# Half-row blocks of 512 columns, a new order of fills, and a fold by transposes in a four-layer transformer kernel

## The chip, the cores and the metric

One NeuronCore of one Trainium2 chip runs the whole program. The metric is the device time of one execution in microseconds; the time of a kernel is the median of its runs. Everything is float32. "TensorE", "VectorE", "ScalarE" and "GpSimd" are the PE, DVE, ACT and POOL of the profile; SP issues the weight transfers.

## The reference

Two blocks of two layers each work on x of 256 tokens by 1024. A layer of the first kind (layers 0 and 1):

```
h = x @ w_in                                  # dq dk dv sq sk sv iq ik iw ga gb
ya = rms_norm(diff_attention(dq, dk, dv, lam))         # 4 heads, two softmaxes each
score = sum_h relu(iq_h . ik) * iw_h                   # index search: 64 keys per query
yb = attention(sq, sk, sv) over the chosen keys        # "dsa", 8 heads
mix = (sigmoid(ga) * (ya @ w_bd) + sigmoid(gb) * (yb @ w_bs)) @ w_o
x = layer_norm(ALPHA * x + mix)
ffn = 2 of 32 experts per token: (silu(x @ w_g) * (x @ w_u)) @ w_d
x = layer_norm(ALPHA * x + ffn + sigmoid(x @ w_ple_gate) * (p @ w_ple))
```

A layer of the second kind (two more):

```
p = rms_norm(x) @ w_in_2                      # cq ckv kr mq mk mv rq rk rv rg g0 g1 g2
o_mla, o_moba = two causal attentions, 8 heads;  o_ret = retention, 4 heads
x = x + (sum of sigmoid(g) * (o @ w_branch)) @ w_out_2
x = x + relu(rms_norm(x) @ w_up)**2 @ w_down
```

The weights are some 420 MB and are read once.

## The kernel before, in words

**One plan, five programs.** `Plan` (L98) writes out the order of all steps; each engine then walks the same list (`for s in plan.steps`) and emits its share of each step, so the order of the plan is the order on every engine and on SP's queue. Within an engine everything is in order; between engines there are semaphores with counted names.

**The weight stream.** The weights are laid out in the order of use, in blocks of up to 128 x 2048 (1 MB). `take` (L163) appends a block: it emits `fetch` (SP's DMA into the next free tile of `self.buffers`) and, for blocks that aren't raw, `split`: ScalarE casts to a high half (L1778), VectorE subtracts it (L1264) to get the low half, each in two pieces of 1024 columns, into one of three pairs WS (`PAIRS`). Splits are emitted up to two blocks ahead. Three ring tiles carry the stream; `lend` (L150) adds a dead tile at the head of the list, with the work that must be over before the first transfer into it, and `recall` takes it back. Before, PT and H are lent when the experts start, GT and V0 from expert 8 on. The experts' down weights are raw: TensorE reads them as float32 from the tile.

**Matmuls.** `mm3` forms each product as three fp32r matmuls (high x high, high x low, low x high). A `tok` step (L945, helper line L916) keeps 128 tokens as the stationary operand and streams 256 columns of w: one block is all eight 128-row slices of 256 columns, one PSUM bank holds both token halves. `gate`, `ret_gate` and `mlp_up` keep the weights stationary and stream 256 tokens. Four banks (`bank_free`: a step waits until the bank used four banks ago is emptied) and scp hold the outputs; `owner` says whether ScalarE or VectorE empties a bank, and `turn` (transposes in groups of four, L993) alternates between them (`either`).

**Fills.** `self.todo` is a list of blocks of TensorE work that wait for nothing (gates, branches); `fill(n)` runs n of them, and `attend` (L231) takes three counts: how many behind the first half's softmax, behind the second's, and before the last product. `self.spare` holds small VectorE steps (index search: 54 per layer; routing; slot weights), of which `pace` are emitted after every `take`.

**A first-kind layer** (L261): iq, ik, sq, sk, then index scores; dq, dk, dv, sv with 9 index steps behind each block; `turn` ST and DT (the transposed q and k); attention "diff"; its output is turned and split (`turn_split` oa, into FA), attention "dsa" follows with the branches and the gates gb as fills; `turn_split` ob, the last branch, `merged` (the sum is split into FA in four pieces, L1526), w_out, `load_p` (the split of p into FA, L1531), norm ln1, ple, `turn_split` ln1, router, ple_gate with the routing behind it, gather, 32 experts. An expert e: two blocks of gate and up weights for 64 tokens, high halves in rows 0 to 63 and low halves in rows 64 to 127 of the stationary operand, so the bank holds 64 high and 64 low rows of 512 outputs; ScalarE copies it (SE, L1920); `turn_h` (L1136) multiplies the copy by the constant "fold" (ones at r and r + 64), which transposes it and adds the two halves in one float32 matmul; ScalarE takes the tanh (L1916), VectorE forms the product (L1686, L1688), and `down` follows under the next expert. `tokens_of` prepares the next expert's tokens (L1913, L1681).

**A second-kind layer** (L392): norm, cq (256 + 160 columns), mq, mk, q_up, kv_up, mv, rv, rq; attentions "mla" and "moba", retention "ret", with gates, ret_gate and branches as fills; `turn_split` o0, o1, o2; the last branch, `merged`, w_out_2, norm, and the MLP in four quarters.

## Time and profile before

| | before |
|---|---|
| median of 3 runs | 2198.76 us (2197.55 to 2204.66) |
| the profiled execution | 2194.55 us, span 2192.7 us |
| mean granted clock of TensorE | 0.954 |
| busy: PE, DVE, ACT, POOL | 93%, 62%, 49%, 5% of the span |
| stream | 421.65 MB in the SP queue, mean 195 GB/s with all else |

The profile gives busy times per engine, what each idle time waited for, and the chain of work that ended last. A wait is put down to the last releaser. Matmul starts are exact; their ends are modelled, so spacings are read from start to start. Most matmuls have the one helper line L916 and are told apart by their tiles: WSh and WSl are the halves of a weight block, XTh and XTl those of the tokens, FA holds split operands, SC the experts' copy and the attention's probabilities. Layers begin near 0, 617, 1227 and 1706 us; experts run from 318 to 588 and from 922 to 1191 us.

### The profile page before, as it was taken

What the parts mean: (1) busy time and instruction counts of PE and PEld (TensorE: products, weight loads), DVE (VectorE), ACT (ScalarE), POOL (GpSimd) and SP (SyncE); (2) the same over time, 40 slices, a digit from 0 to 9 for tenths busy, and PEclk for the clock granted to TensorE, in tenths of its full rate; (3) what the DMA queues carried; (4) which work ended last, traced back from release to release, by engine and by line L of the source; (5) the groups of instructions that cost most, each with busy time, mean ns of one, the idle gap of its engine ahead of it and who ended that gap; (6) DMA issues with size and microseconds to landing.
All of it is one profiled execution on the core that took longest, in us unless ns stands there. A gap on an engine that the chain in (4) does not pass through costs nothing.

```text
span 2192.7 us, 35340 instructions
## 1 busy us (share of the span) xinstructions
PE 2032.7 (93%) x14696; PEld 1920.4 (88%) x14696; DVE 1366.4 (62%) x2230; ACT 1069.1 (49%) x1662; POOL 102.1 (5%) x88
## 2 busy tenths in 40 slices
PE   7979899999989798999999799888999898989998
PEld 7979889999889798899998798888989898988897
DVE  4775668677647756686776555566444655665444
ACT  4443456667534434566675344434444544434443
POOL 1000020000010000200000000000000000000000
PEclk9989889999989998999999799999999999989999
DMA  6423339999624233399996153333555343334552
GB/s 247 155 96 132 111 155 381 392 391 388 233 92 160 96 128 113 150 383 391 389 391 244 58 184 116 105 141 134 181 192 186 136 154 116 127 125 152 192 185 84
DMA packets 60184, 426.95 MB, mean 195 GB/s; under 512 B 6849, under 2 KB 7249, under 8 KB 9200
## 3 DMA queue, kind: packets, MB, share of 16 engines
q1 hardware_dynamic: 59040, 421.65, 52.2%
q8 instruction: 119, 1.95, 0.4%
q0 software_dynamic: 400, 1.75, 0.3%
q10 hardware_dynamic: 576, 1.19, 0.1%
q14 instruction: 49, 0.40, 0.0%
HBM read 423.52 MB, written 1.05 MB: 194 GB/s over the span
## 4 chain that ended last, share of the span: by engine, by line
PE 86%; DVE 8%; ACT 4%; issue 1%; DMA 1%; POOL 0%; DVEq 0%; ACTq 0%; POOLq 0%; SPq 0%
PE bank L916 72%; PE scp L916 10%; DVE WSl L1264 1%; ACT SC L1812 1%; PE bank L1008 1%; PE bank L1035 1%; PE bank L993 1%; ACT WSh L1778 1%; DVE sm L1401 0%; POOL sm L1979 0%; PE bank L1160 0%; DVE scp L1399 0%; DMA ring<-wts 0%; DVE sm L1247 0%; DMA H<-wts 0%
## 5 line engine op out<-in xcount | busy, mean ns | idle before, releaser
L1264 DVE TENSOR_TENSOR WSl<-ring,WSh 128x1024 fp32r<-128x1024 f32 (+3 forms) x560 | 650.5, 1203 | 236.0 <-ACT WSh L1778 234.6
L1778 ACT CAST WSh<-ring 128x1024 fp32r<-128x1024 f32 (+3 forms) x560 | 549.4, 1033 | 178.4 <-PE scp L916 87.7
L916 PE MATMUL bank<-WSh,FA 128*128 128x256 f32 (+1 forms) x1168 | 332.8, 342 | 21.0 <-DVE FA L1526 8.8
L916 PE MATMUL bank<-XTh,WSh 128*128 128x256 f32 x1216 | 348.5, 287 | 0.1
L916 PE MATMUL bank<-XTl,WSh 128*128 128x256 f32 x1216 | 345.4, 284 | 0.0
L916 PE MATMUL bank<-XTh,WSl 128*128 128x256 f32 x1216 | 345.2, 284 | 0.0
L916 PE MATMUL bank<-WSh,XTh 128*128 128x256 f32 (+3 forms) x1024 | 300.9, 294 | 13.8 <-DVE WSl L1264 12.2
L916 PE MATMUL bank<-WSl,XTh 128*128 128x256 f32 (+3 forms) x1024 | 298.3, 291 | 0.0
L916 PE MATMUL bank<-WSh,XTl 128*128 128x256 f32 (+3 forms) x1024 | 297.8, 291 | 0.0
L916 PE MATMUL bank<-WSl,FA 128*128 128x512 f32 (+1 forms) x840 | 297.4, 354 | 0.0
L916 PEld LDWEIGHTS bank<-WSh,FA 128*128 128x128 f32 x1168 | 204.4, 195 | 43.1 <-issue 9.5
L916 PEld LDWEIGHTS bank<-XTh,WSh 128*128 128x128 f32 x1216 | 235.0, 193 | 1.6 <-issue 1.2
L916 PEld LDWEIGHTS bank<-XTl,WSh 128*128 128x128 f32 x1216 | 234.9, 193 | 0.2
L916 PEld LDWEIGHTS bank<-XTh,WSl 128*128 128x128 f32 x1216 | 234.6, 193 | 0.0
L916 PEld LDWEIGHTS bank<-WSh,XTh 128*128 128x128 f32 x1024 | 207.4, 202 | 16.0 <-DVE WSl L1264 12.2
L916 PEld LDWEIGHTS bank<-WSl,XTh 128*128 128x128 f32 x1024 | 207.6, 203 | 0.0
L916 PEld LDWEIGHTS bank<-WSh,XTl 128*128 128x128 f32 x1024 | 207.1, 202 | 0.0
L916 PEld LDWEIGHTS bank<-WSl,FA 128*128 128x128 f32 x840 | 162.9, 194 | 19.2
L916 PE MATMUL bank<-FA,WSh 128*128 128x256 f32 x640 | 129.8, 305 | 32.0 <-DVE FA L1507 14.2
L916 PE MATMUL scp<-WSh,FA 128*128 128x512 f32 x512 | 159.0, 389 | 0.0
L916 PEld LDWEIGHTS bank<-FA,WSh 128*128 128x128 f32 x640 | 110.3, 212 | 35.0 <-issue 31.3
L916 PEld LDWEIGHTS scp<-WSh,FA 128*128 128x128 f32 x512 | 96.1, 188 | 19.7
(263 smaller groups left out, 2853.6 us busy)
## 6 DMA issues: line engine op xcount, KB each, us to landing
ring<-wts SPq DMA_DIRECT2D x296, 1024.0 KB, 4.9
PT<-wts SPq DMA_DIRECT2D x34, 1024.0 KB, 7.3
GT<-wts SPq DMA_DIRECT2D x26, 1024.0 KB, 7.3
H<-wts SPq DMA_DIRECT2D x24, 1024.0 KB, 8.4
V<-wts SPq DMA_DIRECT2D x16, 1024.0 KB, 8.9
ring<-wts SPq DMA_DIRECT2D x2, 768.0 KB, 4.3
ring<-wts SPq DMA_DIRECT2D x2, 640.0 KB, 4.3
X<-x POOLq DMA_DIRECT2D x1, 1024.0 KB, 5.8
```

The costliest lines, as they stand in the source:

```text
L916: return nc.tensor.matmul(dst, lhsT, rhs, start=start, stop=stop)
L993: last = nc.tensor.transpose(bank[u % 4][0:s.w, j * P:(j + 1) * P], src, ident)
L1008: last = nc.tensor.transpose(bank[u % 4][:, j * P:(j + 1) * P], src(t, c), ident)
L1035: last = nc.tensor.transpose(bank[u % 4][:, (j - s.first) * P:(j - s.first + 1) * P], p_at(j // nk)[:, j % nk * P:(j % nk + 1) * P], ident)
L1264: nc.vector.tensor_tensor(lo[:, c], buf[:, c], hi[:, c].bitcast(F32), ALU.subtract).then_inc(*lo_done.inc(("block", i)))
L1778: nc.scalar.copy(hi[:, c], buffers[s.buffer][:, c]).then_inc(*hi_done.inc(("half", i, k)))
L1812: ins = nc.scalar.activation(SC[:, h, 0:kl], scp[:, h, 0:kl], ACT.Exp, bias=nb[t][:, h:h + 1], scale=SCALE[s.name], accum_out=zs[t][:, h:h ...
```

## The change

- `wide`: a group of 512 output columns in two blocks, each four of the eight 128-row slices ("half-row blocks"), into two banks, one per 128 tokens. All `columns`, ple_gate, w_out and cq (416 columns) use it; copies and tanh, and the update of X with its statistics (chunks of 512), follow.
- sv leaves the stretch of the index search and becomes two items of `todo`; `pace` there is 13.
- New counts: dsa (2, 2, 1), mla (2, 1, 1), moba (2, 2, 1); some blocks are kept behind the transposes of ob, o0, o1 and o2.
- `merged` in two halves of its own tiles of FA, w_out starting with the first; `load_p` between the two column groups of w_out, into XT.
- `turn_split` of ln1, ln2 and o2 in groups of two pairs: first both affine steps, then both splits.
- `turn_h` by four transposes; VectorE adds the halves (a reduction out of PSUM into GU) before the tanh.
- YA, YB (QKT), V1 and PT are lent from the second attention of a first-kind layer on; YA and YB come back at expert 1, V1 at expert 27, with waits (`held`) for the last block in them. GpSimd's memset shrinks and its sum into V1 moves to a step `keep`.

```diff
-    def lend(self, name, lender):
+    def lend(self, name, lender, at=0):
         self.lent.add(name)
-        self.buffers.insert(0, (name, lender))
+        self.buffers.insert(at, (name, lender))
+    def wide(self, w, name, l, c, c0, n, src, owner="act", row=None, **fields):
+        u = []
+        def block(h):
+            i = self.take((w, (l if row is None else row,), 4 * h, 4, c0, c0 + n))
+            if h == 0:
+                u.extend(self.bank(owner) for _ in range(T))
+            self.add("wide", name=name, l=l, c=c, h=h, n=n, i=i, u=u, src=src, **fields)
+            self.release(i)
+        return [lambda: block(0), lambda: block(1)]
...
-        self.pace = 9
+        self.pace = 13
         self.columns("w_in", "dk", l, W1["dk"], 512, src)
         self.add("rope", name="dq", l=l)
         self.columns("w_in", "dv", l, W1["dv"], 512, src)
-        self.columns("w_in", "sv", l, W1["sv"], 512, src)
         self.no_more_than(0)
         self.pace = 1
         self.todo.extend(self.gates("w_in", l, "ga", W1["ga"], src))
+        self.todo.extend(self.wide("w_in", "sv", l, 0, W1["sv"], 512, src))
...
-        self.attend("dsa", l, 8, (1, 2, 1), diff_out)
-        self.fill(9)
+        self.attend("dsa", l, 8, (2, 2, 1), diff_out)
+        for name in ("YA", "YB"):
+            self.lend(name, ("pe", "scores", "dsa", l, 1, 1), at=RING)
+        self.lend("V1", ("pe", "attended", "dsa", l, 1), at=RING)
+        self.lend("PT", ("pe", "PT", self.use("PT", "pe") - 1), at=RING)
+        self.fill(len(self.todo) - 1)
         fa = self.use("FA", "pe")
         self.turn_split("ob", l, 4, o=self.now("O"), fa=fa)
-        for f in self.branch("w_branch_dsa", l, "ob", "gb", fa):
-            f()
+        self.fill(9)
+        blocks = self.branch("w_branch_dsa", l, "ob", "gb", fa)
+        blocks[0]()
+        self.add("merged", l=l, stage=1, last="ob", h=0, fa=None)
+        blocks[1]()
         fa = self.use("FA", "pe")
-        self.add("merged", l=l, stage=1, last="ob", fa=fa)
+        self.add("merged", l=l, stage=1, last="ob", h=1, fa=fa)
...
-        self.attend("mla", l, 8, (1, 2, 1))
+        self.attend("mla", l, 8, (2, 1, 1))
         self.turn("MT", l, 16, P)
-        self.fill(9)
+        self.fill(1)
...
-        self.attend("moba", l, 8, (1, 2, 1), mla_out)
-        self.fill(9)
+        self.attend("moba", l, 8, (2, 2, 1), mla_out)
...
-        self.fill(9)
+        self.fill(len(self.todo) - 2)
         fa = self.use("FA", "pe")
         self.turn_split("o2", l, 4, o=o, fa=fa)
+        self.fill(9)
...
-                        last = mm(bank[u % 4][:, f * CAP:(f + 1) * CAP], SE[s.e % 2][:, f * P:(f + 1) * P], const("fold"), True, True)
+                        last = nc.tensor.transpose(bank[u % 4][:, f * P:(f + 1) * P], SE[s.e % 2][:, f * P:(f + 1) * P], ident)
...
+                    both = bank[u % 4][:, :].rearrange("p (f h s) -> p f s h", f=4, h=2)
+                    dve.wait_ge(pe_done, "bank", u)
+                    nc.vector.tensor_reduce(v.rearrange("p g f s -> p (g f) s"), both, AX.X, ALU.add).then_inc(*dve_done.inc(("bank", u), ("folded", l, s.e)))
                     dve.wait_ge(act_done, "silu", l, s.e)
...
-                    act.wait_ge(pe_done, "bank", u)
+                    act.wait_ge(dve_done, "folded", l, s.e)
```

## Rows read from the trace of the kernel before

**Rows 1.** Page, part 1: engine, busy us (share of the span) xinstructions.
```profile
PE 2032.7 (93%) x14696; PEld 1920.4 (88%) x14696; DVE 1366.4 (62%) x2230; ACT 1069.1 (49%) x1662; POOL 102.1 (5%) x88
```

**Rows 2.** Page, part 4: shares of the chain that ended last, by engine.
```profile
PE 86%; DVE 8%; ACT 4%; issue 1%; DMA 1%; POOL 0%; DVEq 0%; ACTq 0%; POOLq 0%; SPq 0%
```

**Rows 3.** Waits of PE: for what; us in total, times, longest us.
```profile
PE bank L916 <- DVE FA L1507: 14.2, 6, 4.9
...
PE bank L916 <- DVE FA L1495: 9.1, 4, 3.0
PE bank L916 <- DVE FA L1526: 8.8, 4, 2.2
PE bank L916 <- DVE FA L1502: 8.8, 2, 4.4
...
PE bank L1008 <- ACT GT L1891: 7.0, 4, 1.9
...
PE scp L916 <- ACT SC L1812: 5.8, 2, 2.9
PE bank L916 <- DVE FA L1531: 4.4, 2, 2.2
```

**Rows 4.** Chain in order of time: start us, us, what, matmuls.
```profile
111.53 1.75 PE bank L993 x16
...
1565.86 23.03 PE bank L916 x192
1588.89 21.79 PE scp L916 x96
```

**Rows 5.** Timeline of PE, cq's 160 columns, first and last of 48.
```profile
1236.57 0.24 PE L916 MATMUL bank<-WSh,XTh 128*128 128x160 f32 x1
...
1241.79 0.28 PE L916 MATMUL bank<-WSh,XTl 128*128 128x160 f32 x1
```

**Rows 6.** Timeline of PE, one expert: start us, us, operation.
```profile
439.50 3.68 PE L916 MATMUL bank<-TMP,V 128*128 128x64 f32 x32
443.01 1.06 PE L916 MATMUL bank<-CST,SC 128*128 128x64 f32 x8
443.88 0.48 PE L916 MATMUL bank<-WSh,FA 128*128 128x512 f32 x1
```

**Rows 7.** Timeline of DVE, a reduction from PSUM.
```profile
123.02 0.69 DVE L1401 TENSOR_REDUCE sm<-scp 128x4 f32<-128x512 f32 x1
```

**Rows 8.** Timeline of DVE in the experts.
```profile
366.14 1.22 DVE L1711 SCALAR_TENSOR_TENSOR X<-GT,X 128x1024 f32<-128x1024 f32 x1
...
441.76 0.68 DVE L1681 TENSOR_TENSOR FA<-A,FA 128x512 fp32r<-128x512 f32 x1
...
444.74 0.29 DVE L1688 SCALAR_TENSOR_TENSOR TMP<-TMP,bank 128x128 f32<-128x128 f32 x1
```

**Rows 9.** Timeline of PE, the expert after those pieces.
```profile
368.02 0.50 PE L916 MATMUL bank<-WSh,FA 128*128 128x512 f32 x1 [0.70 <-DVE FA L1681]
```

**Rows 10.** Stretches of the experts: busy PE, PEld, DVE, ACT, POOL, PEclk, DMA share, GB/s.
```profile
440.00:548.00 108.00, 108.00 (x750) 99.28 (x750) 77.69 (x94) 74.54 (x107) 0.00 (x0) 1.00 0.99 389
380.00:404.00 24.00, 24.00 (x181) 22.54 (x180) 15.62 (x20) 14.51 (x23) 0.00 (x0) 1.00 1.01 418
```

**Rows 11.** Timeline of DVE around the index search of layer 0.
```profile
79.68 2.36 DVE L1264 TENSOR_TENSOR WSl<-ring,WSh 128x1024 fp32r<-128x1024 f32 x2 [6.61 <-ACT WSh L1778]
...
107.37 2.36 DVE L1264 TENSOR_TENSOR WSl<-ring,WSh 128x1024 fp32r<-128x1024 f32 x2 [0.79 <-ACT WSh L1778]
...
112.00 0.69 DVE L1436 COPY A<-bank 128x512 f32<-128x512 f32 x1
```

**Rows 12.** Stretches, columns as in Rows 10.
```profile
318.10:323.10 5.00, 5.00 (x13) 3.84 (x13) 3.48 (x3) 2.28 (x3) 3.60 (x2) 0.50 1.01 426
1310.00:1500.00 190.00, 172.00 (x1377) 167.41 (x1376) 117.30 (x195) 77.05 (x146) 2.03 (x2) 0.96 0.35 123
1790.00:1985.00 195.00, 177.19 (x1397) 172.42 (x1396) 121.26 (x201) 78.81 (x147) 2.04 (x2) 0.94 0.35 124
```

More of the change, by code:

```diff
@@ L67 @@
 C_TABLE = [("ident", 128), ("caus", 128), ("invf", 8), ("iota8", 8), ("nhalf", 8)]
-C1_TABLE = [("before", 128), ("one", 1), ("fold", CAP)]
+C1_TABLE = [("before", 128), ("one", 1)]
 C3_TABLE = [("iota", SLOTS)]
@@ L207, in turn_split @@
     def turn_split(self, name, l, n, at=0, **fields):
-        for j in range(2 * at, 2 * at + n, 2):
-            owner = "act" if name in ("ln1", "ln2", "o2") and j // 2 % 2 == 0 else "dve"
-            self.add("turn_split", name=name, l=l, j=j // 2, n=min(2, 2 * at + n - j), u=self.bank(owner), **fields)
+        pairs = range(2 * at, 2 * at + n, 2)
+        if name not in ("ln1", "ln2", "o2"):
+            for j in pairs:
+                self.add("turn_split", name=name, l=l, j=j // 2, n=min(2, 2 * at + n - j), u=self.bank("dve"), **fields)
+            return
+        for a in range(0, len(pairs), 2):
+            for j in pairs[a:a + 2]:
+                self.add("turn_split", name=name, l=l, j=j // 2, n=2, u=self.bank("dve" if j // 2 % 2 else "act"), **fields)
+            for j in pairs[a:a + 2]:
+                self.add("shifted_split", name=name, l=l, j=j // 2, n=2, **fields)
     def gates(self, w, l, g, c0, src):
@@ L317, in first_layer @@
         for c in range(4):
-            self.add("ple", l=l, c=c, i=i, u=self.bank("act"), gt=gt, fa=fa)
+            self.add("ple", l=l, c=c, i=i, u=self.bank("act"), gt=gt)
         self.release(i)
@@ L332, in first_layer @@
         self.pace = 0
+        blocks = [f for c in range(2) for f in self.wide("w_ple_gate", "ple_gate", l, c, 512 * c, 512, ("ln1", l))]
         for c, self.lead in enumerate((14, 20, 28, 0)):
+            if c == 2:
+                self.first("YA", "YB")
             if c == 3:
@@ L336, in first_layer @@
                 self.add("x_lo", l=l)
-            self.tok("ple_gate", l, c, ("w_ple_gate", (l,), 0, KD, c * 256, (c + 1) * 256), 256, src=("ln1", l))
+            blocks[c]()
             if c == 1:
@@ L1068, in tensor_program @@
                     if s.c == ends:
-                        names += [("read", i)] + ([("FA", s.fa)] if s.kind == "ple" else [])
+                        names.append(("read", i))
                     last.then_inc(*pe_done.inc(*names))
@@ L1265, in vector_program @@
                             *lo_done.inc(("block", i)))
-                elif s.kind == "tok" and s.name == "w_out":
-                    xs = X[:, :, s.c * 256:(s.c + 1) * 256]
-                    dve.wait_ge(pe_done, "bank", u)
+                elif s.kind == "wide" and s.name == "w_out" and s.h:
                     if l < DEPTH:
@@ L1934, in scalar_program @@
                     act.wait_ge(pool_done, "YC0", l)
+                    for block_, raw in plan.held["Y", l]:
+                        if raw:
+                            act.wait_ge(pe_done, "read", block_)
+                        else:
+                            act.wait_ge(lo_done, "block", block_)
                     if s.e:
```

178 lines of the change are left out of this document (112 added, 66 removed).

## Prediction

> **What bounds the kernel now.** I read the page's busy times first, then its chain by engine, the waits of TensorE, and last the timelines where the change cuts. TensorE is busy for 2032.7 of 2192.7 us [rows 1] and holds 86% of the chain that ended last [rows 2]. So a change gains in three ways: fewer microseconds of TensorE work, less idle time before it, and fewer stretches at half clock (the granted clock has two levels here, 1.0 and 0.5 [rows 12]). The idle time is 160 us; its largest removable parts stand in the waits: for the operand splits FA (L1507, L1495, L1526, L1502, L1531), for exp (L1812) and for freed banks (L1891) [rows 3]. Nothing smaller than 0.3% of the time (6.6 us) can be told from no change. The profiled execution took 2194.55 us (span 2192.7), 4.2 us under the median of 2198.76; I sum against it and add 4.2 at the end.
>
> **1. Blocks of 512 columns.** 192 matmuls of 256 columns take 23.03 us, 119.9 ns each; 96 of 512 take 21.79 us, 227.0 ns each [rows 4]. One of 512 replaces two of 256: 12.9 ns saved. A group of 512 output columns has 2 x 8 x 3 = 48 such pairs, 0.62 us. There are 11 groups in a first-kind layer (iq, sq, sk, dq, dk, dv, sv, w_out 2, ple_gate 2) and 7 in a second-kind one (mq, mk, mv, rv, rq, w_out 2): 36 in all, **-22.2 us**. The Trainium skill (TensorE: Matmul & The Clock Gate, Back-to-back issue gap) gives a back-to-back spacing of N/2.4 + 2.5 ns, so a fixed part of 2.5 ns; by it this term would be only 48 x 36 x 2.5 ns = 4.3 us. The rows show 13 ns over the columns' time, so the measurement decides. The copies by ScalarE keep their count of elements; cost nil, under 10.9 us of matmuls.
>
> cq was 256 + 160 columns and becomes 416. The 160-column matmuls start within 5.22 us, 47 intervals of 111.1 ns [rows 5], hardly faster than 256. Before: 48 x (119.9 + 111.1) = 11.1 us. After, between the rows for 256 and 512: 48 x 186.8 = 9.0 us. Two layers: **-4.2 us**.
>
> **2. Fold by transposes.** An expert takes 8.14 us on TensorE: 3.76 us of 512-column matmuls, 3.51 us down, and the fold, 8 records from 443.01 to the next expert at 443.88: 0.87 us [rows 6]. Four transposes replace it; 16 transposes take 1.75 us [rows 4], so 0.44 us. The period becomes 7.71 us if nobody else sets it; 64 x 0.43 = -27.5 us. What it costs VectorE: a reduction of 128x512 from PSUM, nearest row 0.69 us [rows 7]. The chain fold, reduce, tanh, two products grows from about 1.1 to 2.0 us and is hidden under the next expert's 3.76 us. But VectorE is in order: the four split halves and the next tokens are behind it. Now the tokens end at 442.44, 1.44 us before TensorE wants them [rows 8]. Later by 0.95 us and wanted 0.43 us earlier, they have 0.1 us left: TensorE just stays the bound. In experts 3 to 6 VectorE also forms slot weights and adds the ple part (pieces of up to 1.22 us [rows 8]; 1.6, 1.6, 2.4, 2.3 us per expert by the timeline). Today that costs one wait of 0.70 us [rows 9]. Then VectorE needs 4 x 7.0 + 7.7 = 35.7 us for what TensorE does in 30.8: 4.9 us less the slack, 4.5, in place of 0.9 lost now. That is 3.6 us per layer. Bounds of the period: 7.71 (TensorE) and 8.14 (no gain), or above where the reduction is slower than its row. Term: -27.5 + 7.2 = **-20.3 us**.
>
> **3. The stream.** At 7.71 us per expert the 3.15 MB need 408 GB/s. The DMA engines are busy for 0.99 of 440 to 548 us at 389 GB/s, but gave 418 GB/s where more transfers were queued [rows 10]. With eight tiles filled before the experts (three ring tiles, PT, V1, YA, YB, H), 88 of 96 blocks are left: at 389 GB/s 237 us, less than 32 x 7.71 = 247. So the lent tiles hide the roof and give nothing more by themselves: cost nil, bound +20.3 us if they don't. The Trainium skill (DMA: Bandwidth & Descriptors, the table of limits at its head) puts HBM at about 358 GB/s per core; the rows already go beyond that. SP's queue issues the same 402 blocks, and the waits for lenders come behind ring blocks already due. POOL's shorter memset and the later add (V) hide behind experts.
>
> **4. Fills in a first-kind layer.** sv leaves the index search and becomes two items, run while oa is split: the 4.4 us wait (L1502) goes, 8.8 in two layers. A gate block kept behind ob's transposes covers L1507 there (1.1 each, 2.2). Merging by halves lets w_out start after half 0 while branch 1 runs: half of L1526, 4.4. Loading p between w_out's columns takes L1531 away, 4.4 [rows 3]. Grouping ln1's transposes by pairs shortens the chain y, hi, lo; of the L1891 waits (7.0 [rows 3]) and 0.6 before the router I give it 4.8. Sum **-24.6 us**. What is late next: the norm of the diff heads (3.6 us, outside the rows) stays.
>
> The other side: the index search (54 steps) now runs over 4 blocks, not 6. VectorE is in it from 79.68 to its first ST copy at 112.00 [rows 11]. Two splits of 2.28 us fewer (79.68 to the first search step at 81.96) and 0.8 us of idle time less [rows 11] leave 106.7 us. TensorE has 21.8 us of dk and dv from 76.8 (96 x 227.0 ns), then ST's transposes: ready for ga0 at 100.3. ga0's bank is that of ST's first group, whose copy is VectorE's, in order behind the search: free at 107.4. A new wait of 7.1 us, **+14.2 us**. Bounds: nil if that copy fell to ScalarE, 9 us with its own half-clock tail.
>
> **5. Fills in a second-kind layer.** Two blocks, not one, over the exp of mla's first half: L1812, 5.8. A block left behind o0's and o1's transposes, two behind o2's: the rest of L1507 (12.0) and L1495 (9.1). Merging by halves: 4.4. Sum **-31.3 us**. The exp of mla's second half loses one block of cover and still ends under the other.
>
> **6. Clock.** From 1310 to 1500 us the granted clock is 0.96, from 1790 to 1985 it is 0.94 [rows 12]: 7.6 + 11.7 = 19.3 us lost, nearly all just behind the waits of part 5. I take **-16 us** (bounds 0 and 19.3), as the waits under 1 us stay. In a first-kind layer the stall before ga0 replaces the one before the branch: nil.
>
> **Sum.** -22.2 - 4.2 - 20.3 - 24.6 + 14.2 - 31.3 - 16 = -104.4 us. 2194.6 - 104.4 = 2090.2; with 4.2 for the median, 2094.4, say 2094.
>
> **Rivals.**
> (a) *The stream sets the experts' pace.* For it: a DMA share of 0.99 at 389 GB/s. Against: 418 in a backlog, and the lead. Part 2's gain goes: 2094 + 20 = 2114. Chance 0.12.
> (b) *Gaps move instead of closing*: a covered wait reappears at the next join, since ScalarE and VectorE latencies are unchanged. Half of parts 4 to 6 (36 us) goes: 2130. Against: the covers are 5 to 11 us over waits of 1 to 5. Chance 0.10.
> (c) *No stall before ga0*, because the search is over sooner than I count: 2094 - 14, and with its clock about 2072. Chance 0.13.
> (d) *The lent tiles don't run ahead* (a lender's wait blocks SP's queue). The change does not do what it says; experts start with five blocks as now: up to 2114 as in (a). Chance 0.03, counted with (a).
> (e) *Slower than before*: with transposes in each period, TensorE is granted the half clock through the experts. At 0.50, from 318.1 to 323.1 us, 13 matmuls of 512 columns take 5.00 us [rows 12], 0.385 us each for 0.227: 16 x 0.158 x 64 = 162 us, giving 2256. It decides once more than 41 of the 64 experts run at half clock (104 / 2.53). Against: 0.44 us of transposes in 7.7 us is little beside matmuls without a gap, and 16 transposes at 111.53 us ran at 109 ns each. The Trainium skill (TensorE: Matmul & The Clock Gate, Part 4: PE-mode transpose) says that transposes don't count as busy for the clock; this is the rule that would bring it. Chance 0.03.
>
> **How the numbers follow.** The forecast (0.59) spans 2074 to 2116: clock term 0 to 19.3, VectorE's overload 0 to 12. With (a), (b), (c) the range 2064 to 2132 leaves out (e) and the tails. Faster by over 0.3% in all but (e) and an unseen mishap: 0.94; same 0.02; slower 0.04.
>
> **What would show it.** Fold periods of 7.7 us, 8.5 to 9.5 in experts 3 to 6; no waits for oa's splits, for merged and for p; a wait of some 7 us of the first gate block near 100 us; 512-column tok matmuls 227 ns apart; a mean clock near 0.96 to 0.97; TensorE busy about 1965 us, idle for about 125. Wrong if periods stay at 8.1 with DMA waits, if ga0 doesn't wait, or if the clock falls in the experts.

## The result and the profile after

The changed kernel takes 2105.87 us (median; 2105.51 to 2106.41), the kernel before 2198.16 us on the same chip: a ratio of 0.9574, 95% interval 0.9556 to 0.9593. I had forecast 2094 with a range of 2064 to 2132. The sign and the range held; the point was 12 us too low. The profiled execution took 2105.99 us with a span of 2104.2, against 2194.55 and 2192.7 before: 88.6 us less in the executions that the sum was made for, where it said 104.4.

The first part of the page, busy us of each engine, answers to [rows 1]:

```profile
PE 1964.6 (93%) x12616; PEld 1779.6 (85%) x12616; DVE 1410.0 (67%) x2278; ACT 1073.0 (51%) x1662; POOL 94.5 (4%) x88
```

TensorE has 2080 instructions and 68.1 us of busy time less; I had said about 1965 us busy. Its idle time is 2104.2 - 1964.6 = 139.6 us, not the 125 forecast, down from 160. So the busy time came out as summed, though two of its terms were off in opposite directions (see parts 2 and 6 below), and nearly the whole miss of 15.8 us stands in waits. They answer to [rows 3] (for what; us in total, times, longest us):

```profile
PE bank L1071 <- ACT H L1961: 25.2, 4, 9.4
PE bank L968 <- DVE FA L1748: 16.1, 12, 2.8
PE bank L968 <- DVE A L1499: 13.6, 2, 6.8
...
PE bank L1071 <- ACT GT L1968: 7.9, 4, 2.4
...
PE bank L968 <- DVE TMP L1758: 5.9, 4, 1.9
...
PE bank L1071 <- DVE O L1529: 2.6, 2, 1.3
...
PE bank L968 <- DVE GT L1584: 1.7, 2, 0.8
```

Read against [rows 3]: the lines for the splits of oa, of o and o2, of merged, for p and for exp (L1502, L1507, L1495, L1526, L1531, L1812) have no successor, and the largest, for H, had been there at 25.0 us. In place of the closed ones stand two of 6.8 us for A (L1499, ST's copy) that I had forecast as 7.1. But the wait for GT (L1968, once L1891) is 7.9 us where 7.0 had been, and not smaller as forecast, and small new ones follow the closed ones in the second-kind layers (O 1.3, GT 0.8, each twice).

The stall before the first gate block, in the timelines of TensorE and VectorE in layer 0 (start us, us, operation, and the idle time before it). VectorE comes to the copy at 101.52, when its 54 search steps are over, though TensorE, done with ST's transposes, has stood still for 6.79 us before it gets on at 102.36:

```profile
102.36 0.55 PE L968 MATMUL bank<-XTh,WSh 128*128 128x256 f32 x1 [6.79 <-DVE A L1499]
```

```profile
100.76 0.45 DVE L1445 TENSOR_SCALAR TMP<-TMP 128x128 f32<-128x128 f32 x2
101.11 0.50 DVE L1443 TENSOR_TENSOR TMP<-TMP,CST 128x128 f32<-128x128 f32 x2
101.52 1.29 DVE L1499 COPY A<-bank 128x512 f32<-128x512 f32 x2
```

The fold by transposes, TensorE's timeline, answers to [rows 6]. The transposes start at 437.12 and again at 444.75: a period of 7.63 us, where I had 7.71 and before 8.14.

```profile
437.12 0.61 PE L1203 MATMUL bank<-CST,SC 128*128 128x128 f32 x4
441.24 3.68 PE L968 MATMUL bank<-TMP,V 128*128 128x64 f32 x32
444.75 0.61 PE L1203 MATMUL bank<-CST,SC 128*128 128x128 f32 x4
```

Stretches, with the columns of [rows 10]: all experts of layer 0, and the two stretches of the second-kind layers that answer to [rows 12].

```profile
307.98:569.89 261.91, 252.10 (x1689) 227.99 (x1689) 219.41 (x269) 182.06 (x258) 5.00 (x1) 0.99 0.96 387
1300.00:1485.00 185.00, 176.51 (x1374) 169.76 (x1373) 121.37 (x198) 83.09 (x134) 7.50 (x8) 0.98 0.42 146
1755.00:1935.00 180.00, 171.59 (x1325) 165.00 (x1324) 118.40 (x195) 78.40 (x127) 6.46 (x7) 0.97 0.40 143
```

The granted clock in the experts is 0.99: the half clock through transposes, my rival (e), did not come. In the second-kind layers it is 0.98 and 0.97 instead of 0.96 and 0.94.

**What I had not forecast** is one instruction of GpSimd. Its sum into V (L2096) now runs near the end of the experts, and VectorE's instruction beside it, a product that elsewhere takes 0.29 us, takes 3.17. First GpSimd, then VectorE, then TensorE, whose two waits (1.07 and 0.85 us) lengthen two periods from 7.63 to 8.95 and 8.73 us (folds at 505.82, 514.77, 523.50), 2.4 us per layer:

```profile
505.55 5.00 POOL L2096 TENSOR_TENSOR V<-XTh,XTl 128x2048 f32<-128x2048 f32 x1 [198.51 <-DVE WSl L1327]
```

```profile
507.53 3.17 DVE L1756 SCALAR_TENSOR_TENSOR TMP<-TMP 128x128 f32<-128x128 f32 x1 [0.38 <-ACT TMP L1993]
510.74 0.29 DVE L1758 SCALAR_TENSOR_TENSOR TMP<-TMP 128x128 f32<-128x128 f32 x1
```

```profile
511.17 1.08 PE L968 MATMUL bank<-TMP,H 128*128 128x64 f32 x8 [1.07 <-DVE TMP L1758]
516.23 0.50 PE L968 MATMUL bank<-WSh,FA 128*128 128x512 f32 x1 [0.85 <-DVE FA L1748]
```

### The profile page after: what moved, and what is told of

The parts are those of the page before. It is cut to its first block, busy times and chain, and to the rows that moved or that the text cites. A ratio compares the mean times of both kernels' runs of the same rounds, so it can differ in the third digit from the quotient of the medians.

```text
span 2104.2 us, 31210 instructions
## 1 busy us (share of the span) xinstructions
PE 1964.6 (93%) x12616; PEld 1779.6 (85%) x12616; DVE 1410.0 (67%) x2278; ACT 1073.0 (51%) x1662; POOL 94.5 (4%) x88
## 4 chain that ended last, share of the span: by engine, by line
PE 81%; DVE 12%; ACT 4%; issue 1%; POOL 1%; DMA 0%; DVEq 0%; ACTq 0%; POOLq 0%; SPq 0%
PE bank L968 65%; PE scp L968 11%; DVE WSl L1327 3%; PE bank L1071 2%; ACT WSh L1848 2%; PE bank L1203 1%; PE bank L1056 1%; PE bank L1098 1%; DVE sm L1464 1%; ACT SC L1885 1%; POOL sm L2061 1%; DVE scp L1462 0%; DVE TMP L1449 0%; DVE TMP L1441 0%; DVE sm L1447 0%
## 5 line engine op out<-in xcount | busy, mean ns | idle before, releaser
L1327 DVE TENSOR_TENSOR WSl<-ring,WSh 128x1024 fp32r<-128x1024 f32 (+3 forms) x508 | 589.5, 1205 | 236.9 <-ACT WSh L1848 236.0
L1848 ACT CAST WSh<-ring 128x1024 fp32r<-128x1024 f32 (+3 forms) x508 | 497.6, 1034 | 209.0 <-PE bank L968 119.0
L968 PE MATMUL bank<-XTh,WSh 128*128 128x256 f32 x1216 | 351.1, 289 | 13.8 <-DVE A L1499 13.6
L968 PE MATMUL bank<-WSh,FA 128*128 128x512 f32 (+1 forms) x848 | 302.1, 389 | 16.1 <-DVE FA L1748 16.1
L968 PEld LDWEIGHTS bank<-XTh,WSh 128*128 128x128 f32 x1216 | 237.4, 195 | 15.1 <-issue 14.6
L968 PE MATMUL bank<-WSh,XTh 128*128 128x512 f32 (+4 forms) x576 | 227.2, 394 | 13.2 <-DVE WSl L1327 12.3
L968 PE MATMUL bank<-WSl,XTh 128*128 128x512 f32 (+4 forms) x576 | 223.3, 388 | 0.0
L968 PE MATMUL bank<-WSh,XTl 128*128 128x512 f32 (+4 forms) x576 | 223.0, 387 | 0.0
L968 PEld LDWEIGHTS bank<-WSh,FA 128*128 128x128 f32 x848 | 158.0, 190 | 48.8 <-DVE FA L1748 19.6
L968 PEld LDWEIGHTS bank<-WSh,XTh 128*128 128x128 f32 x576 | 118.7, 206 | 33.5 <-DVE WSl L1327 12.3
L968 PEld LDWEIGHTS bank<-WSh,XTl 128*128 128x128 f32 x576 | 118.0, 205 | 19.7
L968 PEld LDWEIGHTS bank<-WSl,XTh 128*128 128x128 f32 x576 | 118.6, 206 | 18.6
```

What stands on the lines that cost most here:

```text
L968: return nc.tensor.matmul(dst, lhsT, rhs, start=start, stop=stop)
L1327: nc.vector.tensor_tensor(lo[:, c], buf[:, c], hi[:, c].bitcast(F32), ALU.subtract).then_inc(*lo_done.inc(("block", i)))
L1848: nc.scalar.copy(hi[:, c], buffers[s.buffer][:, c]).then_inc(*hi_done.inc(("half", i, k)))
```

## The experiments

All start from the changed kernel ("after", 2105.9). Code cuts show the deciding lines of an edit, with "..." where others are left out. Ratios are to the kernel before, whose median lay between 2196.8 and 2198.8 us on each chip.

### 1. Blocks of 512 columns

```diff
-last = mm3(bank[u[t] % 4][:, 0:s.n], cut(lhs, k, slice(t * P, (t + 1) * P)), cut(w, k), c == 0, c == KD - 1)
+for r_ in (slice(0, s.n // 2), slice(s.n // 2, s.n)):
+    last = mm3(bank[u[t] % 4][:, r_], cut(lhs, k, slice(t * P, (t + 1) * P)), cut(w, k, r_),
+               c == 0 and r_.start == 0, c == KD - 1 and r_.start > 0)
```

> Only the width of the matmuls in the steps of 512 columns is undone (the blocks, their transfers, copies and the order of the work stay): each such matmul becomes two of half its columns. The trace's price is 12.9 ns for each of 48 x 36 pairs, 22.2 us, and 48 x (2 x 111.1 - 186.8) = 1.7 us for each cq of 416 columns: 2106 + 22 + 3 = 2131 us. The rival price by a fixed part of 2.5 ns for each matmul: 2106 + 4.3 = 2110 us. A third reading: where the steps cover the work of other engines, wider cover is used up by waits, and less than 22 us comes back (2120 or so).

Measured: 2130.09 us, ratio 0.9697 (0.9670 to 0.9724), 24.2 us over after. Of its span of 2127.0 us TensorE is busy for 1991.0, 26.4 more than in after. The price taken from the rows, 12.9 ns for each pair [rows 4] and 1.7 us for each of the two cq, gives 22.2 + 3.4 = 25.6 us and holds. The fixed part of 2.5 ns by the Trainium skill (TensorE: Matmul & The Clock Gate, Back-to-back issue gap) would have made it 4.3. I had cited that formula as if it were for a stream of matmuls; the section gives it for a single isolated one and says that it doesn't hold in a real kernel's stream, so it was a weak rival.

### 2. The fold

```diff
-last = nc.tensor.transpose(bank[u % 4][:, f * P:(f + 1) * P], SE[s.e % 2][:, f * P:(f + 1) * P], ident)
+last = mm(bank[u % 4][:, f * CAP:(f + 1) * CAP], SE[s.e % 2][:, f * P:(f + 1) * P], const("fold"), True, True)
...
-nc.vector.tensor_reduce(v.rearrange("p g f s -> p (g f) s"), both, AX.X, ALU.add)
```

> Only part 2 is undone: the fold is the product with the float32 constant again, 8 matmuls of 64 columns, and VectorE and ScalarE read the folded bank directly, with no reduction. The theory (the fold by transposes shortened the period from 8.14 to 7.63 us, and gave about 4 us per layer back to VectorE's overload in the experts with spare pieces): the expert period returns to 8.14 us, the waits of TensorE for the tokens nearly go, and the time is 2106 + 64 x 0.51 less 2 to 3 times 4, some 2124 us (2120 to 2130). Rival A (the stream is what sets 7.63 us): the period would stay under 8.0 us and the time under 2112. Rival B (VectorE's overload costs nearly nothing): 2106 + 33 = 2139.

Measured: 2128.18 us, ratio 0.9688 (0.9662 to 0.9715), 22.3 over after. TensorE's timeline of this kernel, folds again 8.14 us apart:

```profile
432.42 1.06 PE L968 MATMUL bank<-CST,SC 128*128 128x64 f32 x8
437.05 3.68 PE L968 MATMUL bank<-TMP,ring 128*128 128x64 f32 x32
440.56 1.06 PE L968 MATMUL bank<-CST,SC 128*128 128x64 f32 x8
```

64 x 0.51 = 32.6 us go up for TensorE, which is what its busy time shows (1997.2 us for 1964.6). 10 to 12 come back as idle time, over 5 per layer: the waits for tokens beside the spare pieces fall from 3.5 us (0.61, 0.78 and 2.13) to 0.70, the 1.9 us that GpSimd's sum costs in waits are gone, since VectorE has time to spare again, and the wait behind the last expert is 1.10, not 1.87. The stream didn't set 7.63 us, or the period would not have followed the fold alone.

### 3. ST's copies: who empties the bank

```diff
-            owner = self.either()
+            owner = "act" if name == "ST" else self.either()
             self.add("turn", name=name, l=l, g=g // 4, first=g, n=min(4, n - g), w=width_, owner=owner, u=self.bank(owner), **fields)
```

> The four groups of transposed index scores ST are all emptied by ScalarE, none by VectorE; nothing else differs. The theory (ga0's matmuls wait only because the first group's bank is emptied by VectorE, in order behind the whole index search): the wait of 6.8 us at 102.36 us goes in both first-kind layers. The search itself isn't longer, so what follows it moves up only as far as TensorE's work, not VectorE, sets the next stage: with the half clock behind the wait 14 to 18 us, giving 2088 to 2092. The rival (the wait only moves: what waits for the search's end, the mask and the diff heads' exp, sets the next start): 2104 to 2107, and a wait of 5 to 7 us appears at the branch or the diff scores behind it.

Measured: 2090.96 us (2089.10 to 2091.84), ratio 0.9515 (0.9489 to 0.9541): 14.9 us less than after, as expected (2088 to 2092), and the lowest median of the study. So it is shown that the stall hung on which engine empties that bank. What is left of the wait is at the scores of the diff heads (TensorE's timeline), which again wait for a copy behind the search, but after ga0's 48 matmuls:

```profile
105.01 2.08 PE L968 MATMUL scp<-A 64*128 64x128 f32 x16 [2.28 <-DVE A L1499]
```

Layer 0's first expert starts at 297.83, not 307.98, layer 1's at 880.86, not 895.05: 10.2 us, then 4.0 more. Of each, 4.5 are the wait (6.79 - 2.28) and 0.9 the one for PT behind it (1.73, now 0.79); what is left, +4.7 in one layer and -1.4 in the other, is in no wait. Half clock accounts for the first: ahead of layer 0's experts TensorE is busy for 265.5 us, in after for 270.5, with the same 1594 matmuls. The rival that the wait only moves holds for a third of it: 2.28 of 6.79.

### 4. Where sv stands

```diff
-        self.pace = 13
+        self.pace = 9
...
+        self.columns("w_in", "sv", l, W1["sv"], 512, src)
...
-        self.todo.extend(self.wide("w_in", "sv", l, 0, W1["sv"], 512, src))
...
-        self.attend("dsa", l, 8, (2, 2, 1), diff_out)
+        self.attend("dsa", l, 8, (1, 2, 1), diff_out)
```

> The one edit of sv is undone: its blocks stand in the index search again (6 blocks at 9 pieces each, not 4 at 13), and the second attention has one fill after its first half, as before. My theory: dk, dv and sv give TensorE 10.9 us more before ST's transposes, so that the stall before ga0 (6.8) goes, while VectorE's search grows by about 3 us (a split of 2.3 and 0.8 idle) and the 4.4 us wait for oa's splits returns: 2106 - 2 x 6.8 + 2 x (4.4 + 3) + 0 to 2 = 2106 to 2110. The rival (the moved block simply pays where it is covered: the stall was cheap and the half clock behind oa costs more): 2114 or more. The other (the stall costs more than the wait it replaced): 2095 to 2102.

Measured: 2107.22 us (2104.62 to 2113.61), ratio 0.9582 (0.9557 to 0.9608): 1.4 us over after, not to be told from no change. The stall before the gate block is 0.46 us, that block starts 5.0 us later (107.33 for 102.36), and the wait for oa's splits is back (two waits of 4.4):

```profile
107.33 0.36 PE L968 MATMUL bank<-XTh,WSh 128*128 128x256 f32 x1 [0.46 <-DVE A L1499]
```

```profile
PE bank L968 <- DVE FA L1569: 8.7, 2, 4.4
```

In waits the old place is even the better one: two of 6.8 us go but for 0.46 each, two of 4.4 come, and TensorE's idle time is 134.9 us (2111.8 - 1976.9), 4.7 less than in after. Its busy time is 12.3 us longer for the same 12616 instructions, in a profiled execution that lies 6.4 us over the median; that is half clock, and it takes the gain back. So the move of sv by itself closed one wait, opened a longer one and gained nothing that can be told. With experiment 3 the wait for oa's splits stays closed and a third of the stall is left.

### 5. The fills of the second-kind layers

```diff
-        self.attend("mla", l, 8, (2, 1, 1))
+        self.attend("mla", l, 8, (1, 2, 1))
...
-        self.fill(1)
+        self.fill(9)
...
-        self.attend("moba", l, 8, (2, 2, 1), mla_out)
+        self.attend("moba", l, 8, (1, 2, 1), mla_out)
+        self.fill(9)
...
-        self.fill(len(self.todo) - 2)
+        self.fill(9)
```

> In the second-kind layers the fills and splits are those of the kernel before: exp of mla's first half covered by one block, one step of o0's and o1's transposes followed by 9 fills' time as before, nothing kept back behind o2's; merging by halves stays. The theory of parts 5 and 6: the waits for exp (5.8), o (12.0) and o2 (9.1) return, 27 us, with most of the half clock behind them, 12 to 16: 2106 + 41 = 2147 (2140 to 2150). A rival (the clock isn't tied to these waits): 2133. Another (the fills only move waits elsewhere; before and after differ mainly by width): under 2125.

Measured: 2143.50 us, ratio 0.9739 (0.9702 to 0.9777), 37.6 over after. Two of the three waits are back, 12.0 for o and 5.8 for exp as in [rows 3], and the third at 7.1 of 9.1; the granted clock falls with them (waits of TensorE, then two stretches):

```profile
PE bank L969 <- DVE FA L1575: 12.0, 4, 4.9
PE bank L969 <- DVE FA L1563: 7.1, 4, 3.2
PE scp L969 <- ACT SC L1886: 5.8, 2, 2.9
```

```profile
1310.00:1500.00 190.00, 174.13 (x1309) 167.05 (x1309) 116.31 (x192) 78.27 (x127) 6.46 (x7) 0.95 0.37 132
1765.00:1950.00 185.00, 169.21 (x1281) 161.92 (x1281) 117.01 (x199) 77.93 (x136) 3.34 (x4) 0.95 0.37 131
```

The three waits make 24.9 us, less the 4.3 us of small ones that stood in their place: 20.6. The other 17 of 37.6 are clock: TensorE's busy time is 17.2 us longer (1981.8 for 1964.6) with the same 12616 instructions, nearly one us for each us of waiting. The rival of a clock untied to the waits (2133) falls.

### 6. Merging by halves, and the place of p

```diff
         blocks[0]()
-        self.add("merged", l=l, stage=1, last="ob", h=0, fa=None)
         blocks[1]()
+        self.add("merged", l=l, stage=1, last="ob", h=0, fa=None)
...
-            if c == 0:
+            if c == 1:
                 self.add("load_p", l=l, xt=self.now("XT"))
```

(the same in the second-kind layers, stage 2 and o2).

> Half 0 of the merged branches is split only after both blocks of the last branch, in all four layers, and p is loaded behind both columns of w_out in the first-kind layers. By the terms of parts 4 and 5: the wait for merged's second split returns in part, 2.2 in each of four layers (8.8), and the wait for p, 2.2 in each of two (4.4): 2106 + 13 = 2119 (with half clock behind them up to 2123). The rival (the waits were covered anyway, since with blocks of 512 columns half 0 of w_out takes 10.9 us, not 5.8): 2106 to 2110.

Measured: 2123.47 us, ratio 0.9659 (0.9634 to 0.9684), 17.6 over after. Its waits, for merged's splits and for p:

```profile
PE bank L968 <- DVE FA L1593: 9.1, 4, 2.3
PE bank L968 <- DVE XTl L1598: 4.3, 2, 2.2
```

13.4 us of waits for the 13.2 of the terms. But they aren't the whole balance. In this kernel one of the two waits for GT in each layer is gone, and one before the router, like before's of 0.6 us, is back:

```profile
PE bank L1071 <- ACT GT L1968: 4.8, 2, 2.4
PE bank L968 <- DVE XTl L1562: 1.6, 2, 0.8
```

That is 3.1 us less and 1.6 more, which makes 11.9, and TensorE's idle time is 11.9 us over after's. The wait for p stands right ahead of ple's matmuls and so of the transposes that wait for GT; the edit undoes two things, but by this order it is the early load of p that opens a wait for GT where it closes its own. TensorE's busy time is 9.0 us over after's with the same 12616 instructions, half clock, so that the time lies at the top of what was expected.

### 7. The grouping of ln1's transposes

```diff
             for j in pairs[a:a + 2]:
                 self.add("turn_split", name=name, l=l, j=j // 2, n=2, u=self.bank("dve" if j // 2 % 2 else "act"), **fields)
-            for j in pairs[a:a + 2]:
                 self.add("shifted_split", name=name, l=l, j=j // 2, n=2, **fields)
```

> The transposes of ln1, ln2 and o2 go back from pairs of two (turn, turn, split, split) to one after the other (turn, split, turn, split); the order of the other work stays. My prediction gave the pairing 4.8 us; the trace of after shows waits of 1.54 and 2.42 us there, as much as before (1.90, 1.75). Theory now: the wait is for banks that ScalarE empties, behind its cast of a weight block of 2.0 us, whatever the grouping: 2104 to 2108. Rival (the pairing does give 2.4 per layer and hides a loss from elsewhere): 2111.

Measured: 2116.51 us, ratio 0.9628 (0.9603 to 0.9653), 10.6 over after. My theory is wrong: the grouping works, and the rival (2111) is nearer. The line for GT grows:

```profile
PE bank L1070 <- ACT GT L1967: 11.8, 4, 4.4
```

That is 3.9 us, and ScalarE's timeline shows how. Without the grouping its second cast of XTh waits 1.85 us for VectorE's affine step, and ple's copy stands behind it in order, at 254.20 us; in after the copy comes at 252.84, with no such wait (this kernel, then after):

```profile
253.67 0.62 ACT L1924 CAST XTh<-TMP 128x512 fp32r<-128x512 f32 x1 [1.85 <-DVE TMP L1546]
254.20 1.06 ACT L1967 COPY GT<-bank 128x512 f32<-128x512 f32 x2
```

```profile
251.80 1.14 ACT L1925 CAST XTh<-TMP 128x512 fp32r<-128x512 f32 x2
252.84 1.06 ACT L1968 COPY GT<-bank 128x512 f32<-128x512 f32 x2
```

This isn't all of before's order (there a block of ple's output stood behind each single pair), so it shows that in the new order of work the grouping is needed, not that it gained over before, where the line was 7.0 [rows 3] and is 7.9 in after. Other waits add 1.0. The rest of the 10.6 is half clock: TensorE's busy time is 8.2 us longer with the same 12616 instructions. Part of it is in the same 88 or 89 matmuls from the ranks to the first expert, between the same waits, in after and in this kernel:

```profile
284.50:307.98 23.48, 20.31 (x88) 16.14 (x88) 15.21 (x30) 10.40 (x15) 6.50 (x4) 0.93 0.23 88
```

```profile
286.87:313.55 26.68, 23.51 (x89) 18.19 (x89) 15.21 (x30) 10.41 (x15) 6.50 (x4) 0.80 0.31 122
```

The clock's share is 3.2 us here, in a stretch the edit doesn't touch, some 30 us behind the wait that it lengthens. Experiment 9 has the like.

### 8. The lent tiles, and GpSimd's sum

Two kernels take lending back. The first takes all four tiles (PT is lent at the experts again), the second leaves V1 lent:

```diff
-        for name in ("YA", "YB"):
-            self.lend(name, ("pe", "scores", "dsa", l, 1, 1), at=RING)
-        self.lend("V1", ("pe", "attended", "dsa", l, 1), at=RING)
-        self.lend("PT", ("pe", "PT", self.use("PT", "pe") - 1), at=RING)
...
+        self.lend("PT", ("pe", "PT", self.use("PT", "pe") - 1))
```

> YA, YB and V1 aren't lent to the stream in a first-kind layer's second attention, and PT is lent at the experts only, as in the kernel before; everything else is as after. My theory of part 3 (the lead is worth nothing by itself at this period: the stream gives 401 to 418 GB/s where transfers are queued): 2106 to 2110. The rival (the lead hides the roof of 375 to 390 GB/s; at 7.63 us for 3.15 MB the experts want 412 GB/s): without four tiles of 262 KB the last experts fall behind, 4 blocks x 0.67 us = 2.7 us per first-kind layer at the least and, if the roof of 375 GB/s holds, up to 32 x (8.39 - 7.63) - the lead left, some 15 to 20 us per layer: 2111 to 2145.

Measured: 2119.22 us (2111.96 to 2120.98), ratio 0.9640 (0.9607 to 0.9673): 13.3 over after, not nil. But not by the stream. (The rival's least cost was put too low: the blocks have 1024 KB each, not 262, so four of them take 10.8 us at 389 GB/s, not 2.7.) From 380 to 550 us TensorE doesn't idle at all, periods are 7.63 us, and no expert waits for a transfer:

```profile
380.00:550.00 170.00, 170.00 (x1165) 155.34 (x1165) 143.06 (x178) 125.13 (x177) 0.00 (x0) 1.00 1.00 412
```

The loss is mostly before the first expert. With V1 not lent, GpSimd's sum may start as soon as its multiplications are done; it begins 0.2 us ahead of VectorE's sum of the first tokens (0.69 us elsewhere) and holds it to its own end. Timelines of GpSimd, VectorE, TensorE:

```profile
308.34 4.50 POOL L2093 TENSOR_TENSOR V<-XTh,XTl 128x2048 f32<-128x2048 f32 x1
```

```profile
308.57 4.82 DVE L1745 TENSOR_TENSOR FA<-A,FA 128x512 fp32r<-128x512 f32 x1 [5.81 <-ACT FA L1987]
```

```profile
313.44 0.79 PE L965 MATMUL bank<-WSh,FA 128*128 128x512 f32 x1 [6.83 <-DVE FA L1745]
```

6.83 us of waiting for 2.70 in after, and half clock behind it: the first fold comes 7.7 us later than in after. At the end of the experts 2.4 us come back. The second kernel was made to part the two causes:

> As the kernel without lent tiles, but V1 is lent from the second attention on, so that GpSimd's sum into V comes at the end of the experts as in after; YA and YB aren't lent and PT only at the experts. The first theory, formed from the trace without lent tiles (its expert periods were 7.63 us with no wait for a transfer; all of its 13 us came from the sum at 308.34 us holding VectorE's token sum): 2105 to 2108 us, first expert near 308 us. The rival (the lead of four tiles is worth something in the stream itself): 2110 to 2119, with waits for blocks in the last experts.

Measured: 2114.07 us (2112.78 to 2115.94), ratio 0.9613 (0.9577 to 0.9649). Both readings missed the number, and the trace says why. The stream again sets nothing (periods of 7.63 us up to 522.58 and from 536.02 on). The sum came at 520.05 and fell on two halves of a split (2.36 us elsewhere):

```profile
519.88 6.67 DVE L1325 TENSOR_TENSOR WSl<-GT,WSh 128x1024 fp32r<-128x1024 f32 x2
```

```profile
527.21 0.80 PE L966 MATMUL bank<-WSh,FA 128*128 128x512 f32 x1 [4.02 <-DVE FA L1746]
```

One expert took 13.44 us, in layer 1 another 14.58. Over 7.63 that is 5.8 and 7.0, where after loses 2.4 twice: 8.0 more, and 2105.9 + 8.0 = 2113.9. So what the stream gains from YA, YB and the early PT can't be seen, beyond that it moves the sum from 505.55 to 520.05 us; what the sum costs hangs on which of VectorE's instructions it meets. Of the 5.8 and 7.0 us, 4.0 each are the wait and the rest is half clock behind it. These sums were read off two layers of one execution each, so their closeness to the median is in part chance.

### 9. Pieces: of the sum, and of VectorE's spare work

```diff
-nc.gpsimd.tensor_tensor(XA, XT[0][:, :, :].bitcast(F32), XT[1][:, :, :].bitcast(F32), ALU.add)
+for k in range(KD):
+    nc.gpsimd.tensor_tensor(XA[:, k, :], XT[0][:, k, :].bitcast(F32), XT[1][:, k, :].bitcast(F32), ALU.add)
```

> GpSimd's sum into V, one instruction of 5.0 us, becomes 8 of one eighth each; nothing else differs. The theory (VectorE's next instruction doesn't get on before GpSimd's running instruction ends: a 0.29 us product took 3.17 us beside the sum in after, and the 0.69 us token sum 4.82 us in the kernel without lent tiles): with pieces of 0.6 us no instruction of VectorE is held by more than about 0.7 us, the two long periods of 8.95 and 8.73 us shrink to 7.7 to 8.0, and 1.5 to 2.4 us per first-kind layer come back: 2101 to 2103 us. The rival (the two engines share the port for as long as GpSimd has work, pieces or not): the long periods stay and the time is 2106; with more fixed cost on GpSimd, 2106 to 2108.

Measured: 2113.75 us (2110.55 to 2120.38), ratio 0.9613 (0.9583 to 0.9642). Neither: it is worse. The eight pieces take 9.01 us for 5.00, and each VectorE instruction with two operands beside them is held by a piece. Four halves of splits, 4.62 us in after, take 6.76:

```profile
508.10 9.01 POOL L2097 TENSOR_TENSOR V<-XTh,XTl 128x256 f32<-128x256 f32 x8 [199.92 <-DVE WSl L1327]
```

```profile
509.01 0.69 DVE L1754 TENSOR_REDUCE TMP<-bank 128x256 f32<-128x512 f32 x1 [0.40 <-PE bank L1203]
510.08 0.67 DVE L1756 SCALAR_TENSOR_TENSOR TMP<-TMP 128x128 f32<-128x128 f32 x1 [0.38 <-ACT TMP L1993]
511.43 6.76 DVE L1327 TENSOR_TENSOR WSl<-ring,WSh 128x1024 fp32r<-128x1024 f32 x4
```

The long expert now loses 5.3 us (12.92 for 7.63), where after loses 2.4; in two layers that is 5.7 of the 7.9 us. But TensorE waits hardly longer: once for 2.24 us, where in after it waits for 1.07 and 0.85. The other 3.0 us of the long expert are half clock behind that one wait: the granted clock is 0.74 in it, while in after's two long periods it stays 1.00. So the pieces bring nothing in waits, as they lengthen the sum, and lose by gathering two short waits into one that the clock falls behind.

The reduction, with its one operand in PSUM, isn't held. The Trainium skill (SBUF — State Buffer, SBUF: two separate sides) says that VectorE and GpSimd share one pair of ports, taken as an exclusive lock for a whole instruction, by VectorE where both its inputs lie in SBUF against a GpSimd instruction that reads SBUF. The kernels here agree with it, in who is held and in that more instructions mean more turns of waiting. They agree too in that the first one goes on: in after VectorE's token sum began 0.16 us before GpSimd's (505.39 for 505.55) and took its usual 0.69, while GpSimd's took 5.00, not 4.50. I had not applied it in part 3, where I had let the sum hide behind experts.

```diff
+            if 2 <= e <= 20 and e % 2 == 0:
+                self.spread_out(1)
...
-            if e == 7:
+            if e == 21:
                 self.no_more_than(0)
```

(the lending of GT and V0 moves from expert 8 to 22.)

> VectorE's ten spare pieces (slot weights and the ple part) come one in every second expert from 2 to 20 instead of three per expert from 3 to 6; the turn of the slot weights and the lending of GT and V0 come behind them. The theory of part 2's overload (an expert leaves VectorE 1.1 us of idle time, less 0.4 that is a wait for TensorE; a piece of up to 1.22 us fits in two experts): the periods of 8.49, 8.68, 11.62 and 10.41 us become 7.63 except for the one with the turn, and with the half clock of 3.4 us in them 5 us per layer come back: 2094 to 2098 us. The rival (the piece is in VectorE's order ahead of the tokens, so each one late costs its excess all the same): ten periods of 7.9 to 8.3 us, 2102 to 2108. Against both: GT and V0 come to the stream later; if it needed them, waits for transfers appear and it is slower.

Measured: 2104.26 us (2097.94 to 2107.94), ratio 0.9564 (0.9526 to 0.9603): not to be told from after, and not the 2094 to 2098 that I expected. Periods didn't all become 7.63 us: in layer 0 two are 7.78, three 8.31 to 8.32, and the one with the turn 10.22. The experts did get shorter, by 3.7 us per layer (first fold to last: 245.23 for 248.95), and the waits for tokens fell from 16.1 to 11.6 us. But in layer 0 the last expert's product with its down weights, the same 33 instructions, now falls at half clock (stretches of this kernel, then of after):

```profile
561.78:569.61 7.83, 7.06 (x33) 6.88 (x33) 0.59 (x2) 0.59 (x1) 0.00 (x0) 0.50 0.60 251
```

```profile
564.14:569.89 5.75, 4.98 (x33) 4.79 (x33) 0.59 (x2) 0.59 (x1) 0.00 (x0) 0.70 0.80 335
```

2.1 us go there, 1.4 before layer 0's experts (they begin at 309.34, not 307.98), and 1.7 between layer 0's second norm (589.67 for 589.75) and layer 1's experts (896.63 for 895.05), in stretches that the edit doesn't touch. Of 7.4 us 5.2 are gone so, and the span is 1.9 us shorter. Together with experiment 3:

> Two edits together: ST's four groups emptied by ScalarE, and the ten spare pieces one in every second expert. If both hold as measured apart (2105.9 - 15 = 2091 for the first; the second made the experts of the trace 3.7 us shorter per first-kind layer and gave 4 us back to half-clock stretches behind them, 2104.3): 2085 to 2090 us. If the half clock behind the experts takes all of the second's gain: 2091. It has no claim on more: the wait of 2.3 us for the mask and the diff heads' waits remain.

Measured: 2091.76 us, ratio 0.9506 (0.9482 to 0.9530), the same as experiment 3 alone.

## Why the prediction was right, and where it was not

The forecast held, and so did the mechanisms of most of its terms; one step of part 3 and one term of part 4 failed. The sum for the profiled execution missed by 15.8 us; the 4.2 us added for the median hid part of that, since the changed kernel's profiled execution lies only 0.1 us from its median.

**Part 1, width: right.** -26.4 forecast, 26.4 us of TensorE's busy time and 24.2 of the total when undone. The price from this kernel's own rows, 12.9 ns, was five times the 2.5 of the formula that I set beside it, and held.

**Part 2, fold: right in sum, with two sizes off.** -20.3 forecast, 22.3 when undone. The period is 7.63, not 7.71: from the fold to the next expert's first matmul it is 0.37 us, where I had 0.44, and TensorE saves 32.6 us, not 27.5. VectorE's excess beside the spare pieces cost 3.5 us of waits per layer where I had 4.5, but with the half clock behind the longest wait it cost more in the periods. In layer 0 they are 8.49, 8.68, 11.62 and 10.41 us, 8.7 over four of 7.63; in before they were 8.14, 8.14, 9.03 and 10.73, 3.5 over four of 8.14. That is 5.2 us where I had 3.6. The 8.5 to 9.5 that I had forecast for all four left out that the turn of the slot weights stands in the last of them.

**Part 3, stream: the right answer for the stream, and the step that failed beside it.** "The later add (V) hides behind experts" is wrong. None of the rows that I had read showed an instruction of GpSimd holding VectorE, and I took both engines as independent. It costs 2.4 us per layer, 4.8 in all. Lending V1 matters all the same, in a way I didn't see: it keeps the sum away from the start of the experts, where it costs 4.1 us of waits per layer (6.83 for 2.70), not 1.9.

**Part 4, first-kind fills.** The stall before ga0 came as worked out: 6.8 for 7.1, in the place named, for the cause named (experiment 3); both of its ends came 5 us earlier than I had them (101.52 for 106.7 us and 95.6 for 100.3), which left the difference. The move of sv, forecast at +14.2 - 8.8 = 5.4 us, costs 13.6 - 0.9 - 8.7 = 4.0 us in waits, and nothing that can be told in the time (experiment 4). Merging by halves and p's place held (13.2 forecast in parts 4 and 5, 13.4 in waits and 17.6 in time when undone). The term that failed is ln1's: -4.8 forecast on 7.6 (7.0 for GT and 0.6 before the router), and 7.9 is left. The grouping does shorten the chain (experiment 7), but the chain alone doesn't end the wait: TensorE waits for the banks of ple's output, which ScalarE empties in order, the first ones after a cast of a weight block of 1.98 us, the next ones after its share of the first group, 1.02 and 1.14 us. And loading p early, a term of its own, brought TensorE there sooner: where p comes late, 3.1 of the 7.9 us are gone (experiment 6; that p is the cause is read from the order of the work, not tested apart). That is rival (b), on a small scale.

**Part 5, second-kind fills.** All named waits went. I had written for exp that it "still ends under the other" and nothing for the rest; behind the closed waits stand 1.31 us for O (L1529) and 0.84 for GT (L1584) in each layer, 4.3 us. It is rival (b) again, at an eighth of its size.

**Part 6, clock.** -16 forecast. From the stretches: 185 x 0.02 + 180 x 0.03 = 9.1 us still lost, for 19.3 before, so -10. The whole kernel says the same: of the 68.1 us of busy time that went, 26.4 are the width's and 32.6 the fold's by experiments 1 and 2, which leaves 9.1. So the term was some 6 us too large. Undoing the fills in the changed kernel costs 17 us of clock, near to what I had, so what the fills are worth in clock depends on the kernel that they are taken from. That TensorE's busy time came out at 1965 as forecast is luck: the fold gave 5 more and the clock 7 less.

The misses in waits are 3.8 (sum) + 5.1 (ln1) + 4.3 (second kind) = 13.2 of the 14.6 us of idle time that came over the forecast.

**Not settled.** The single undoings add up to 24.2 + 22.3 + 37.6 + 17.6 + 10.6 + 1.4 = 113.7 us, the whole change gives 92.3. Each undoing was measured in a kernel tuned around it, and part of each is half clock that falls where it falls. I did not run the parts alone from the kernel before, so which pieces overlap stays open; nor did I try the sum on another engine, or a kernel in which it meets no instruction of VectorE with two SBUF operands. What half clock each edit causes, and what of it only falls elsewhere by chance, the runs don't part either.

## What to carry to other kernels

Ask of each new fill which engine empties the banks in front of it, and what else stands ahead on that engine: two copies in each first-kind layer, given to ScalarE, were worth 15 us, a sixth again of the whole change. Move work between engines only after looking at both timelines together, since an instruction on a third engine can stretch one of an engine that TensorE waits for, without any semaphore. And price by rows of the kernel's own trace, but read a gain of less than some 5 us from the waits and periods: the total moves by as much through where the half clock falls.

## What the runs showed of the hardware

- A GpSimd sum with both operands in SBUF held each VectorE instruction with two SBUF operands that came after it had begun until it ended: 0.29 us became 3.17, 0.69 became 4.82, 2.36 became 6.67. One that had begun 0.16 us before the sum kept its 0.69 us, and the sum took 5.00 us for 4.50. A reduction from PSUM beside it kept its 0.69 us. Cut into eight, the sum took 9.01 us, not 5.00; TensorE then waited once for 2.24 us, with a granted clock of 0.74 over that expert, where it had waited 1.07 and 0.85 at 1.00. GpSimd's multiplication by a constant holds less: in the kernel before VectorE's token sum beside it took 0.97 us for 0.69 (timelines of GpSimd and VectorE):

```profile
315.98 5.72 POOL L2012 TENSOR_SCALAR X<-X 128x1024 f32<-128x1024 f32 x2
```

```profile
316.59 0.97 DVE L1681 TENSOR_TENSOR FA<-A,FA 128x512 fp32r<-128x512 f32 x1 [4.75 <-ACT FA L1913]
```

  There the rule of a full lock in the Trainium skill (SBUF — State Buffer, SBUF: two separate sides) goes further than the trace: the token sum ran 0.61 us after the first multiplication, of 2.9 us, had begun and ended well before it, as far as the profile's rough spans of GpSimd can tell.
- Four transposes in each expert's period left the granted clock at 1.00 over 170 us, at a period of 7.63 us (380 to 550 us of the kernel without lent tiles).
- In the same stretch the DMA engines gave 412 GB/s at a busy share of 1.00, with the three ring tiles and H, PT, GT and V0 lent, and TensorE didn't wait.
- The same stretch of some 88 matmuls with the same waits took 23.48 us at a mean granted clock of 0.93 and 26.68 at 0.80 in two kernels that don't differ in it (experiment 7).
